# Token tiles skewed across the norms, four split slots on two raw slots, unrolled feed-forward loops, in a two-layer hybrid encoder

## The reference, cut to what matters

```
x = LN(alpha*x + 0.5*SwiGLU_1(x))                 # 1024 -> 2*2816 -> 1024
x = LN(alpha*x + (sum_n sigmoid(x G_n + c_n) * (mixer_n W_br[n])) W_out)
x = LN(alpha*x + 0.5*SwiGLU_2(x))
x = LN(alpha*x + sigmoid(x W_g + b_g) * (p W_p))
```

## Time and profile before

| what | value |
|---|---|
| median of 3 runs | 1507.65 us |
| profiled execution | 1508.07 us, span 1506.3 us |
| TensorE busy | 1445.1 us, 96% of the span |
| VectorE, ScalarE busy | 980.7 us, 665.0 us |
| chain that ended last | PE 89%, DVE 8%, DMA 1%, ACT 1%, issue 1% |
| DMA | 262.96 MB, mean 175 GB/s |

### The profile page before, as it was taken

The page is one execution under the profiler, slowest core; times in us unless marked ns, Lnnn a source line. Parts: engine busy times, 40 slices in busy tenths (PEclk is TensorE's granted clock), DMA queues, the critical chain, the costliest instruction groups (busy, mean ns, idle before and its releaser), DMA issues.

```text
span 1506.3 us, 24801 instructions
## 1 busy us (share of the span) xinstructions
PE 1445.1 (96%) x10362; PEld 1360.7 (90%) x10362; DVE 980.7 (65%) x1091; ACT 665.0 (44%) x649; POOL 53.2 (4%) x102
## 2 busy tenths in 40 slices
PE   8999989999999899999789999899999998999996
PEld 8999979999999799998689999799999997999974
DVE  4544477889786854445764445678897867545466
ACT  4443434844545444434343444357435454444432
POOL 5000000000000200000000000000000001000000
PEclk9999989999999999999989999899999999999998
DMA  9655535455535576564556555345455546555541
GB/s 322 199 176 192 190 112 169 139 196 170 176 109 191 181 219 194 171 193 166 167 173 194 193 182 181 112 168 168 168 168 168 166 154 207 181 190 186 190 134 66
DMA packets 168028, 262.96 MB, mean 175 GB/s; under 512 B 8958, under 2 KB 101456, under 8 KB 167952
## 3 DMA queue, kind: packets, MB, share of 16 engines
q1 hardware_dynamic: 163616, 249.66, 51.0%
q0 software_dynamic: 4336, 12.20, 2.7%
HBM read 260.77 MB, written 1.05 MB: 174 GB/s over the span
## 4 chain that ended last, share of the span: by engine, by line
PE 89%; DVE 8%; DMA 1%; ACT 1%; issue 1%; SPq 0%; DVEq 0%; ACTq 0%
PE ps L1240 27%; PE ps L1242 27%; PE ps L1241 27%; PE ps L1469 3%; DVE big L886 2%; DVE big L822 2%; PE ps L1273 1%; PE ps L1275 1%; PE ps L1280 1%; DVE xtok L827 1%; DVE big L846 1%; DVE stats L833 1%; DMA raw<-in_ffn_w_in 1%; PE ps L1398 1%; DVE wlo L758 1%
## 5 line engine op out<-in xcount | busy, mean ns | idle before, releaser
L758 DVE TENSOR_TENSOR wlo<-raw,whi 128x2048 fp32r<-128x2048 f32 x230 | 524.9, 2289 | 344.9 <-ACT whi L532 344.7
L532 ACT CAST whi<-raw 128x2048 fp32r<-128x2048 f32 x230 | 438.3, 1908 | 525.6 <-PE ps L1242 482.1
L1240 PE MATMUL ps<-xhi,whi 128*128 128x256 f32 x2272 | 643.9, 283 | 3.4 <-DVE S L773 3.2
L1242 PE MATMUL ps<-xhi,wlo 128*128 128x256 f32 x2272 | 641.3, 282 | 0.0
L1241 PE MATMUL ps<-xlo,whi 128*128 128x256 f32 x2272 | 640.8, 282 | 0.0
L1240 PEld LDWEIGHTS ps<-xhi,whi 128*128 128x128 f32 x2272 | 429.3, 189 | 5.8 <-DVE wlo L758 3.4
L1241 PEld LDWEIGHTS ps<-xlo,whi 128*128 128x128 f32 x2272 | 429.6, 189 | 1.7
L1242 PEld LDWEIGHTS ps<-xhi,wlo 128*128 128x128 f32 x2272 | 429.2, 189 | 0.0
L1242 PE MATMUL ps<-whi,hid 128*128 128x512 f32 x352 | 138.9, 395 | 0.0
L1240 PE MATMUL ps<-whi,hid 128*128 128x512 f32 x352 | 138.8, 394 | 0.0
L1241 PE MATMUL ps<-wlo,hid 128*128 128x512 f32 x352 | 138.8, 394 | 0.0
(11 more groups left out here) (238 smaller groups left out, 1311.4 us busy)
## 6 DMA issues: line engine op xcount, KB each, us to landing
raw<-in_ffn_w_in SPq DMA_DIRECT2D x172, 512.0 KB, 4.7
raw<-in_w_in SPq DMA_DIRECT2D x140, 512.0 KB, 4.6
raw<-in_ffn_w_out SPq DMA_DIRECT2D x88, 512.0 KB, 4.2
raw<-in_w_br SPq DMA_DIRECT2D x32, 512.0 KB, 4.8
raw<-in_w_out SPq DMA_DIRECT2D x16, 512.0 KB, 4.8
raw<-in_ple_gate_w SPq DMA_DIRECT2D x16, 512.0 KB, 4.8
g_bc<-in_ln_g POOLq DMA_DIRECT2D x8, 512.0 KB, 4.5
b_bc<-in_ln_b POOLq DMA_DIRECT2D x8, 512.0 KB, 5.8
```

Of the source, the lines that this page charges most:

```text
L532: nc.scalar.copy(whi[:, slot, :], raw[:, slot, :]).then_inc(whi_made, 1)
L758: nc.vector.tensor_tensor(wlo[:, slot, :], raw[:, slot, :], whi[:, slot, :].bitcast(F32), ALU.subtract).then_inc(wlo_made, 1)
L1240: nc.tensor.matmul(dst, a_hi, b_hi, start=start, stop=False, skip_group_check=True)
L1242: return nc.tensor.matmul(dst, a_lo, b_hi, start=False, stop=stop, skip_group_check=True)
```

## The change

- **Rings.** RING = 4 slots for `whi` and `wlo`, RAWS = 2 for `raw`. SyncE may load chunk c when `wlo` of chunk c - 2 is made; ScalarE may cast chunk c when chunk c - 4 is used. The `his` and `los` calls reach one chunk further in most places.
- **Last chunks by tile.** At the end of a feed-forward the last three `down` stand in the order tile 0 of blocks 8, 9 and 10, then tile 1 of 8 and 9, then `turn_x` of tile 0, then tile 1 of 10; the last gate_up chunks are loaded ahead of their down chunks (`gu_at`, `wo_at`). The output projection and the embedding's gate are skewed in the same way.
- **First block in token order.** The first block behind a norm is `fresh_tokens(t)`: stationary x of one tile, 512 moving weight columns, 24 matmuls a tile. Tile 0 runs, then `turn_x` of tile 1, then tile 1. For a feed-forward the block's hidden values then lie by token, and four transposes (`turn_hidden`) turn them, between the halves of gate_up(1). The input projection begins with C_V, which was seventh; `input_forget` is three narrow passes on the split x, 24 matmuls a tile.
- **Norms.** `normalise(t)`, `los` and `low_x(t)` follow each tile's statistics; the quarters of norms 2 and 4 go by tokens.
- **Loops.** All feed-forward loops are written out.

```diff
-RING = 3
+RING = 4
+RAWS = 2
-GROUPS = [D_G, D_A, A_X, A_Y, C_Q, C_K, C_V, C_O, B_Q, "kv"]
+GROUPS = [C_V, D_G, D_A, A_X, A_Y, C_Q, C_K, C_O, B_Q, "kv"]
...
+                sp.wait_ge(wlo_made, c - RAWS + 1)
...
+                slot, source = c % RING, c % RAWS
+                act.wait_ge(raw_full[source], 32 * (c // RAWS))
+                if c >= RING:
+                    act.wait_ge(chunk_used, c - RING + 1)
...
@@ ScalarE, ffn
+                for j in range(NFF):
+                    n, g = n0 + j, c0 + gu_at(j)
+                    his(g + RING + (j > 0))
                     act.wait_ge(gate0_done, n + 1)
                     nc.scalar.activation(sil[:, 0, :], ps[:, 0, 0:256], ACT.Silu).then_inc(silu_made, 1)
+                    if j == 0:
+                        his(g + RING + 1)
+                    act.wait_ge(chunk_used, g + 2)
                     nc.scalar.activation(sil[:, 1, :], ps[:, 1, 0:256], ACT.Silu).then_inc(silu_made, 1)
...
@@ ScalarE, before the embedding's gate
+                his(base + AT_PW + 2)
+                split_x(4 * l + 3, 0)
                 his(base + CHUNKS)
+                split_x(4 * l + 3, 1)
...
@@ VectorE, ffn
+                for j in range(NFF):
+                    n, g = n0 + j, c0 + gu_at(j)
+                    los(g + RING + (j > 0))
+                    product(n, 0)
+                    if j == 0:
+                        los(g + RING + 1)
+                    product(n, 1)
...
@@ VectorE, norm, behind a tile's bn_aggr
+                        normalise(t)
+                        if last or (i == 3 and t == 0):
+                            continue
+                        los(following + 2 + t)
+                        low_x(nn + 1, t)
+                los(following + 4)
...
@@ VectorE, steps
-                    los(base + gate_chunk(s, 1) + 3)
+                    los(base + gate_chunk(s, 1) + RING)
...
-                    los(base + gate_chunk(s, 1) + 4)
+                    los(base + gate_chunk(s, 1) + RING + 1)
...
@@ TensorE, ffn
+                fresh_tokens(c0, 0, 0, version, n0 == 0, signal=gate0_done)
+                if n0 > 0:
+                    turn_x(version, 1, xtok)
+                fresh_tokens(c0, 1, 1, version, n0 == 0)
...
+                gate_up(NFF - 1)
+                for j in range(NFF - 3, NFF):
+                    down(j, 0)
+                for j in range(NFF - 3, NFF - 1):
+                    down(j, 1)
...
+                turn_x(version + 1, 0, xtok)
+                down(NFF - 1, 1)
...
@@ TensorE, embedding
+                gate(0, 0, 0)
+                turn_x(nn + 3, 1, xtok)
+                gate(0, 1, 0)
+                gate(1, 0, 0)
+                gate(1, 1, 0)
+                gate(0, 0, 1)
+                gate(0, 1, 1)
+                gate(1, 0, 1)
                 if l + 1 < DEPTH:
+                    turn_x(nn + 4, 0, xtok)
+                gate(1, 1, 1)
```

More of the change, by code:

```diff
@@ L562, in ffn @@
[L562 to L570, removed]
+                    if j == 0:
+                        his(g + RING + 2)
+                        if middle is not None:
+                            middle()
+                        act.wait_ge(h0_T, n0 // NFF + 1)
+                        nc.scalar.copy(hhi[0], ps[:, 3, :].rearrange("p (q t) -> p q t", q=2)).then_inc(hhi_made, 1)
+                    else:
+                        act.wait_ge(h_made, 2 * n + 2)
+                        nc.scalar.copy(hhi[j % HIDS], hf).then_inc(hhi_made, 1)
+                        his(g + RING + 2)
@@ L777, in group @@
                                             ALU.subtract).then_inc(hlo_made, 1)
-                los(c0 + 4)
-                c = made[0]
-                group(n0, 0)
-                if middle is not None:
-                    middle()
-                with dve.Fori(0, (NFF - 1) // 2) as j:
-                    for u in range(2):
-                        lo(c + 3 * u, 2 * j)
-                        lo(c + 3 * u + 1, 2 * j)
-                        group(2 * j + (n0 + 1 + u), (1 + u) % 2)
-                        lo(c + 3 * u + 2, 2 * j)
@@ new lines, in low_x @@
+            def low_x(n, t):
+                for g in range(2):
+                    dve.wait_ge(xhi_made, 4 * n + 2 * t + g + 1)
+                    cols = slice(PAD + P * t, PAD + P * t + P)
+                    nc.vector.tensor_tensor(xlo[:, 4 * g:4 * g + 4, cols],
+                                            ps[:, 2 + 2 * t + g, :].rearrange("p (k t) -> p k t", k=4),
+                                            xhi[:, 4 * g:4 * g + 4, cols].bitcast(F32), ALU.subtract).then_inc(xlo_made, 1)
@@ L1228, in embedded @@
                     residual(t, c, e)
-                norm(l, 3, [(t, c, lambda a=a, t=t, c=c: embedded(a, t, c)) for a, (t, c) in enumerate(BY_COLUMNS)],
-                     base + CHUNKS + 2)
+                    if a == 2 and l + 1 < DEPTH:
+                        los(base + CHUNKS + 2)
+                        low_x(4 * l + 4, 0)
+                norm(l, 3, [(t, c, lambda a=a, t=t, c=c: embedded(a, t, c)) for a, (t, c) in enumerate(BY_TOKENS)],
+                     base + CHUNKS)
         @block.tensor
@@ L1295, in cm_chunk @@
+            def cm_chunk(c, kk, bank, bh, bl, first=True, last=True):
                 chunk_ready(c)
@@ L1363, in gate_up @@
                         ins.then_inc(chunk_used, 1)
[L1365 to L1372 removed]
+                        if j == 1 and kk == 0:
+                            turn_hidden()
@@ L1421, in _ @@
             pe.wait_ge(ident_in, 16)
-            turn_x(0, xtok)
+            for t in range(TT):
+                pe.wait_ge(x_in[t], 16)
+                turn_x(0, t, xtok)
             keep_busy(8)
```

517 lines of the change are left out of this document (234 added, 283 removed).

## The result

The changed kernel takes 1562.9 us in the median of 4 runs (1560.5 to 1566.9), the kernel before 1506.95 on the same chip (1505.5 to 1509.1): ratio 1.0364 [1.0347, 1.0382]. It is slower, as forecast, but by 56 us instead of 30, and outside the range (1500 to 1556). The profiled execution took 1560.45 us, 52.4 more than that of before.

The account below looks back on a forecast made before the run. TensorE, busy 96% of the span, was the bound; only its idle time could be had. Terms: -15.6 - 3.3 + 4.0 + 0.2 + 13 + 10.4 + 3.0 + 18.4 = +30 on 1508.07: 1538 us, range 1500 to 1556.

Parts of the forecast that it names:

- norms 1 and 5: Into the input projection: both TensorE waits for VectorE go; each gains 7.8 us (5 to 10.5), -15.6.
- tail: Last norm, after the last matmul: one tile follows it instead of two, -3.3 us.
- norm 2: Feed-forward start behind it: 8.6 us wait, chunk loaded beside gains and next layer's small parameters; +4.0 us (-4.5 to +6).
- norm 6: Feed-forward start behind it, without next layer's parameters: wait 4.7 us, in all 7.1 for 6.9; +0.2 us (-4.5 to +2).
- start of the kernel: First feed-forward: chunk 4 lands late beside other loads, TensorE waits 11.1 us; +13 us with transposes and half clock.
- norms 3 and 7: Into the embedding: third gate chunk split late, wait 8.5 us, half clock 2.0; +5.2 us each, +10.4.
- norm 4: Waits there, a 5.4 us wait at the next feed-forward's start and half clock: 14.9 us for 11.9, +3.0 (-6 to +5).
- mixers: Mainly step 5: late third low part, TensorE waits 8.3 us for the square; 9.2 us a layer, +18.4 in all.
- The trip: Raw chunk through two slots: load, cast, low part become serial, 9.4 us from one low part to the one after next.
- The loads come in time: Rival, whole kernel: the fourth split slot replaces the third raw slot, only gains stand; 53 us faster, 1455 us; chance 0.10.
- More of it: Rival, mixers' steps 1 to 4: late arrivals stall TensorE too (sig or pt), 3 us in 5 places, 1553 us; chance 0.18.
- The trips count only where no other load is near: Rival: gains' loads don't delay chunks, VectorE is not late at step 5; -10, 1498 to 1512 us, middle 1505; chance 0.14.

Follow-up runs that it names:

- three-slot kernel: The changed kernel with three raw slots instead of two, room made in other buffers: 1470.15 us, ratio 0.9757 to the kernel before.

## Why the prediction was wrong

For each term: the time from every matmul's start to the next, less the median of its shape (0.119 us for 256 columns, 0.232 for 512), summed over the stretch, after less before, with the own time of the matmuls that one of the two has more. All terms give 52.6 us, the two executions 52.4. A single term can shift by about 1 us with the place where its stretch is cut.

| term | predicted | measured |
|---|---|---|
| norms 1 and 5 | -15.6 | -10.9 |
| tail | -3.3 | -3.9 |
| norm 2 | +4.0 | +2.4 |
| norm 6 | +0.2 | -1.2 |
| start of the kernel | +13 | +12.1 |
| norms 3 and 7 | +10.4 | +11.6 |
| norm 4 | +3.0 | 0 |
| mixers | +18.4 | +42.5 |

- *The trip.* Right: 9.4 us, its load 5.2 (measured 5.3), and the places where it comes through: 7.93 for a forecast 8.6 at norm 2, 3.95 for 4.7 at norm 6, 8.2 for 8.5 at norms 3 and 7. The three-slot kernel shows what the gains are worth where the loads do come in time: 1470, and 1461 with most of its waits removed, for the 1455 of the rival *The loads come in time*.
- *Norms 1 and 5.* The gaps went, but about 2 us less was won at each. The narrow matmuls now stand in two groups of 24 and half clock followed each, 3.4 to 3.5 us long, 1.7 lost each time; 0.9 had been taken for both.
- *Norm 4.* The wait in the feed-forward behind it was 2.72 instead of 5.4, and that is the difference.
- *Start of the kernel.* Near in number by luck: one wait of 11.1 us was forecast; there were two, of 3.99 and 4.49, each with half clock behind it, so the gap of 5 to 9 us named as a sign did not come there. The other signs came.
- *Mixers: the step that failed.* The step-5 part was right: the wait for the square 7.03 (forecast 8.3), and 1.86 us more before the mean's matmuls, each with half clock behind, lose 15.6 us a layer with the transition before them, for 6.3 before the change: about 9 more; 8.5 was forecast. Step 7 lost 1.3 and 1.6 for 0.7. What failed is that the sum held nothing for the steps ahead of step 5: "VectorE reaches the taps later" was followed to the taps alone. I followed the late chunk through VectorE's program and not through ScalarE's, where two things that TensorE waits for stand behind a cast. In the first layer the query evacuation does, shown by ScalarE's timeline:

```profile
344.37 1.90 ACT L540 CAST whi<-raw 128x2048 fp32r<-128x2048 f32 x1 [7.00 <-DMA raw<-in_w_br]
346.17 1.56 ACT L581 ACTIVATE S<-ps,pc 128x256 f32<-128x256 f32 x4
```

  The cast waits 7.00 us for a load that SyncE issued at 339.34, right behind a low part; the evacuation behind it is done at 347.7, and TensorE starts at 347.79 after 3.81 idle. From there to 353.6 it runs at half clock, 2.9 lost: 6.7 in all. At 429.69 it is the pt copies, 3.03 and 2.9: 5.9. So 12.6 in the first layer. In the second the pt copies cost 5.9 again, but the query evacuation only 2.7, because full clock followed its wait (TensorE's timeline, then a window behind it):

```profile
1118.68 0.39 PE L1245 MATMUL ps<-xhi,whi 128*128 128x256 f32 x1 [2.41 <-ACT S L581]
...
1118.60:1122.00 3.40, 3.32 (x28) 3.33 (x29) 3.40 (x5) 2.56 (x4) 0.00 (x0) 1.00 0.02 5
```

  That makes 21 us in two layers that stood in no term. They are most of the 24 us by which the mixers exceed their term (42.5 for 18.4), and so of the whole miss (1562.9 against 1538); the other terms together came out 1 to 2 us below their forecast. The run that holds back the mixers' loads alone confirms the size of the whole term from outside: 43.6 us over a kernel whose mixers lose 23 us, as those of the kernel before do.
- *The rivals.* "More of it" had just this mechanism, "for sig or pt", at 3 us in each of 5 places, and 0.18. It was right in kind, and too small: it named pt but not the query evacuation, and priced five places at 15 us where four cost 21 (6.7, 5.9, 2.7 and 5.9), since half clock nearly doubled three of the waits. It took the range to no more than 1556, 7 us short. The rivals of loads in time and of lone trips are refuted for two slots; unrolling is worth nothing. The sum of the rival *The trips count only where no other load is near* does not come out: its terms and the gains of 15.6 and 3.3 give -13, 1495, not -10 and not a middle of 1505; by its own terms it lay below the range.

What stays open: why half clock follows some groups of narrow matmuls and not others, and some waits of 2 to 3 us and not others, even within one kernel. No run told that apart.

## What to carry to other kernels

Before a staging buffer is cut, write down the trip that becomes serial, and then look in the program of *every* engine on the trip for what is queued behind it: each such instruction that the bottleneck waits for is a term. Price each wait of the bottleneck with the half clock that may stand behind it; here waits of 2.8 to 3.8 us cost 5.9 to 6.7, and one of 2.4 cost 2.7. The order of the programs is worth trying even while the chunks are late: with two slots it won 38 of the 93 us, at the starts of the feed-forwards and at the embedding. But where an engine's next work is queued behind the late chunk again, as in the mixers, it mostly gives the wait another name, and only the third slot removed it.

## What was not expected of the hardware

- Groups of 24 matmuls of 8 columns were followed by 3.4 us at a granted clock of 0.50 although TensorE was not idle (223.8 and 234.1 us of the changed kernel), and in the kernel with the feed-forwards' starts reordered the clock stayed at 1.00 around and behind the same groups of the first layer (there 214.9 to 217.7 and 223.2 to 226.0 us), while it fell to 0.50 behind one of the two of the second layer (986 to 988 us).
- Fifty matmuls of 256 columns in a wait of 7 us, 6.15 us of work with no use, did not make the kernel slower and raised the granted clock behind the wait from 0.50 to 0.71 in one layer and to 1.00 in the other: 3 us less were lost there.
- A wait of 1.86 us (465.51 us of the changed kernel) had 3.4 us at a granted clock of 0.50 behind it, one of 2.41 us (1118.68) had full clock.
